# Five weight halves whose low part is a sum made by an accumulating transfer instead of a subtraction on VectorE

## The chip, the core and the metric

The kernel runs on one core of a Trainium2 chip. The metric is the device time of one execution in microseconds. The core has TensorE (matrix products; PE in the profile), VectorE (DVE), ScalarE (ACT), GpSimd (POOL), and SyncE (SP), whose queue issues nearly all transfers. Engines run their own lists of instructions in order and wait for one another only at semaphores.

## The reference

One block of a hybrid encoder: 512 tokens of width 1024, all in float32. A normalised input goes through one wide projection; three branches work on its columns (A, a matrix memory with four heads; B, sparse attention with eight heads; M, attention into 256 memory tokens), and their outputs are merged:

```python
merged = (g[:, :, 0] * (y_a @ w_branch[l, 0])
          + g[:, :, 1] * (y_b @ w_branch[l, 1])
          + g[:, :, 2] * (y_m @ w_branch[l, 2]))
x = x + merged @ w_out[l]
```

The change lies in the products `y_m @ w_branch[2]` and `y_b @ w_branch[1]`.

## The kernel before, in words

**Products in two parts.** TensorE takes operands of a shorter format (fp32r). To keep the precision, each operand is split: the high part is the operand rounded to that format, the low part is what is left. Each product of float32 matrices is then three products: high by high, high by low, low by high. For weights, `w_raw` receives the columns from memory, ScalarE copies them into `w_hi` (`split_hi`, L1472 to L1480), and VectorE subtracts, `w_lo = w_raw - w_hi` (`split_lo`, L2230 to L2234).

**Panels and halves.** A panel is 1024 rows by 512 columns of weights, in two halves `kh` of 512 rows (128 partitions by 2048 elements, 1 MB). `w_raw`, `w_hi` and `w_lo` have one slot for each `kh`. TensorE takes a half in four blocks of 12 products each (`panel`, L830 to L849) and waits ahead of it for the semaphore `w_lo_done`, which counts the low parts in the order of all halves. A slot of `w_hi` and `w_lo` comes free when TensorE has finished the same `kh` of the panel before (`w_used` for kh 0, `proj_done` for kh 1); so while TensorE works on one half, the other is prepared.

**The stage of the change.** After the pairs of B heads come four branch panels, `GB[0]` to `GB[0] + 3`: two for M, two for B. They are called panels 0 to 3 here, and their halves (0,0), (0,1), (1,0) and so on to (3,1). Ahead of panel 0 and in panels 0 to 2, TensorE also does pieces of the last two B heads. Behind each panel VectorE multiplies the four results by gates and adds them up (`branch_merge`, L2737 to L2747). SP loads the next panels (`load`), each half once the low part that was made from the same slot is done, and behind panel 3 it waits for all eight low parts (L757) before it loads the first weights of branch A.

**GpSimd in the stage.** Its last work for B is a power at about 505 us. Then it waits for `ys_lo` to reach `2 * KT`, that is for the low parts of all of B's outputs, and makes four sums of token blocks, `s_full` (L3224 to L3231); the last of eight instructions raises `s_made`. Behind them stand the sums of weights for branch A (`weight_sums`).

**Branch A's first head.** TensorE begins with four operands for queries and keys (`queries_keys`), numbered 0 to 3 here, and goes on with the unit products, operands 4 to 10. Each operand is split as above, by `operand_high` on ScalarE and `operand_low` on VectorE. ScalarE's order in the first head (`a_body`, L2036 on) is: operand 1, a wait for `s_made`, the high part of one sum (`sums_high`, L2033), operand 2, another sum, operand 3, two more sums, then the evacuation `first_tap(0)` (L2000), operand 4 and so on. VectorE's order is: operands 0 to 3 with the merge of panel 3 behind operand 0, the convolution of what `first_tap` left (L2813), operand 4, low parts of the sums (L2874), operands 5 and 6, more convolutions, a sum, operand 7 (L2801).

Of the kernel before, what the change touches and what calls it, by code (L numbers as in the profile page):

```python
# [10 lines left out]
ALU = mybir.AluOpType  # L11
ACT = mybir.ActivationFunctionType
# [9 lines left out]
MT = MEM // P  # L22
# [93 lines left out]
GB = _plan.take(4, 4, (4,) * 4)  # L116
# [40 lines left out]
def hybrid_block(nc, x, mem, positions, norm_g, mem_norm_g, w_in, conv_w, conv_b, mlstm_gate_b,  # L157
# [3 lines left out]
    with ctx:  # L161
        def sb(name, shape, dt=F32):
            return ctx.enter_context(nc.sbuf_tensor(name, shape, dt))

        def sem(name):
            return ctx.enter_context(nc.semaphore(name))
# [4 lines left out]
        w_raw = sb("w_raw", [P, 2, KH, S])  # L171
        w_hi = sb("w_hi", [P, 2, KH, S], F32R)
        w_hi_at = nc.sbuf_base - 4 * 2 * KH * S
        w_lo = sb("w_lo", [P, 2, KH, S], F32R)
# [173 lines left out]
        small2 = sb("small2", [P, 52])  # L348
# [14 lines left out]
        half_turned, half_hi, half_lo = sem("half_turned"), sem("half_hi"), sem("half_lo")  # L363
# [2 lines left out]
        small_landed, vec_landed, ang_landed = sem("small_landed"), sem("vec_landed"), sem("ang_landed")  # L366
        w_landed, idx2_landed = [sem("w_landed0"), sem("w_landed1")], sem("idx2_landed")
        w_hi_done, w_lo_done, w_used = sem("w_hi_done"), sem("w_lo_done"), sem("w_used")
        w_first_cast, w_first_hi, w_first_lo = sem("w_first_cast"), sem("w_first_hi"), sem("w_first_lo")
        idx2_hi_done, idx2_lo_done = sem("idx2_hi_done"), sem("idx2_lo_done")  # L370
        proj_done = [sem(f"proj_done{b}") for b in range(4)]
        bank_empty = [sem(f"bank_empty{b}") for b in range(4)]
# [43 lines left out]
        vec_cols = sem("vec_cols")  # L416
# [395 lines left out]
        def _(pe):  # L812
# [99 lines left out]
            def k_transposes():  # L912
                pe.wait_ge(k_parts, 2)
                pe.wait_ge(gate_steps, 3)
                pe.wait_ge(vec_cols, 2)
                for c in range(2):
                    for t in range(TT):
                        ins = turn(att[1 + c][:, t * P:(t + 1) * P],
                                   k_pair[:, t, c].rearrange("p d n -> p (d n)"), ident[:, :])
                    ins.then_inc(idx_turned, 1)  # L920
# [65 lines left out]
            def first_products(c, m, k0, k1, high=(), low=(), mem_low=(), weights_last=True):  # L986

                orders = (((0, 0), high), ((1, 0), mem_low), ((0, 1), low))
                if not weights_last:
                    orders = (orders[0], orders[2], orders[1])  # L990
                for j, ((a, b), wait) in enumerate(orders):
                    if wait:
                        pe.wait_ge(*wait)
                    for k in range(k0, k1):
                        ins = mm(banks[2 * c + m][:, :], memT[a][:, k, m * P:(m + 1) * P], (w_hi, w_lo)[b][:, c, k % KH, :],
                                 start=(k == 0 and j == 0), stop=(k == KT - 1 and j == 2))
                return ins

            pe.wait_ge(w_first_cast, 1)
            first_products(0, 0, 0, 1, (half_hi, 1), (w_first_lo, 1), (half_lo, 1), weights_last=False)  # L1000
            turn_tile(1)
            first_products(0, 0, 1, 2, (w_first_hi, 1), (w_first_lo, 2))
# [466 lines left out]
        def _(act):  # L1469
            A_ = nc.scalar.activation  # L1470
            steps = Steps(act, act_step)

            def split_hi(p, kh, loads, n, before=None):

                act.wait_ge(w_landed[kh], loads * 16)
                if kh == 1 and before is not None:
                    act.wait_ge(proj_done[before[0]], before[1])
                elif kh == 0 and not (isinstance(p, int) and p == 0):
                    act.wait_ge(w_used, p)
                A_(w_hi[:, kh, :, 0:n], w_raw[:, kh, :, 0:n], ACT.Copy).then_inc(w_hi_done, 1)  # L1480

            def split_y(src, tiles=range(KT)):
                for k in tiles:
                    A_(y_hi[:, k, :], src[:, k * S:(k + 1) * S], ACT.Copy).then_inc(ys_hi, 1)
# [211 lines left out]
            def m_evac(h, first):  # L1696
                for e in range(2):
                    act.wait_ge(proj_done[e], h + (MS[2][e] + 1))
                    if first and e == 0:
                        act.wait_ge(vec_cols, 3)  # L1700
                        act.wait_ge(km_norm_steps, 9)
                    A_(m_qh[:, e, :], banks[e][:, :], ACT.Copy, scale=gqk[:, e:e + 1])
                    A_(m_qfull[:, e, :], banks[e][:, :], ACT.Copy, scale=gqk[:, e:e + 1])
                    ins = A_(m_sq[:, e, :], banks[e][:, :], ACT.Square)
                    ins.then_inc(bank_empty[e], 1)
                for e in range(2):
                    b = 2 + e
                    act.wait_ge(proj_done[b], h + (MS[2][b] + 1))
                    if not first and e == 0:
                        act.wait_ge(m_y, h * 2)  # L1710
                    A_(m_zs[:, e, :], banks[b][:, :], ACT.Silu).then_inc(bank_empty[b], 1)
# [70 lines left out]
            def b_values_high(a):  # L1782

                act.wait_ge(u_added, 6 * (a // 2) + (2 if a % 2 else 6))
                if a:
                    act.wait_ge(b_out, a)
                for half in range(2):
                    ins = A_(b_vh[:, 2 * half:2 * half + 2], b_rawT[a % 2][half][:, :, 2 * P:3 * P], ACT.Copy)
                ins.then_inc(b_vhigh, 1)

            def b_probs_high(a):
                ph = b_pT[0][:, :].rearrange("p (b n) -> p b n", n=P)
                if a % 2 == 0:
                    act.wait_ge(b_rotated, a + 2)
                for t in range(TT):
                    act.wait_ge(b_pturned, a * 4 + (t + 1))
                    if t == 0 and a:
                        act.wait_ge(b_out, a)
                    A_(ph[:, t:4 * t + 1:3, :],
                       att[(t + 2) % 4][:, 0:(t + 1) * P].rearrange("p (s n) -> p s n", n=P), ACT.Copy)\  # L1800
                        .then_inc(b_phigh, 1)

            def b_qk_high(a):
                if a:
                    act.wait_ge(b_scores, 4 * a)
                act.wait_ge(b_turned, a * 2 + 1)
                A_(b_qT[0][:, :], att[0][:, :], ACT.Copy).then_inc(b_qhigh, 1)
                act.wait_ge(b_turned, a * 2 + 2)
                A_(b_kT[0][:, :], att[1][:, :], ACT.Copy).then_inc(b_khigh, 1)
# [110 lines left out]
            split_hi(GB[0] + 1, 0, GB[1] + 2, 512)  # L1920
            b_probs_high(r)
            split_hi(GB[0] + 1, 1, GB[1] + 2, 512, (3, GB[2][3] + 1))
            b_values_high(l)
            b_qk_high(l)
            b_exps(l)
            split_hi(GB[0] + 2, 0, GB[1] + 3, 512)
            b_probs_high(l)
            for k in range(KH):
                yb_high(k)
            split_hi(GB[0] + 2, 1, GB[1] + 3, 512, (3, GB[2][3] + 2))  # L1930
            for k in range(KH, KT):
                yb_high(k)
            split_hi(GB[0] + 3, 0, GB[1] + 4, 512)
            split_hi(GB[0] + 3, 1, GB[1] + 4, 512, (3, GB[2][3] + 3))

            def raw_of(n, first):
                if n == 1 and first:
# [287 lines left out]
        def _(dve):  # L2225
            V = nc.vector
# [3 lines left out]
            def split_lo(p, kh, n):  # L2230

                dve.wait_ge(w_hi_done, p * 2 + (kh + 1))
                V.tensor_tensor(w_lo[:, kh, :, 0:n], w_raw[:, kh, :, 0:n], w_hi[:, kh, :, 0:n].bitcast(F32),  # L2233
                                ALU.subtract).then_inc(w_lo_done, 1)  # L2234
# [73 lines left out]
            V.tensor_copy(memg_col, att[2][:, 0:KT]).then_inc(memg_cols, 1)  # L2308
            dve.wait_ge(memg_cols, 2)
            dve.wait_ge(piece_landed[0], 16)  # L2310
            V.tensor_copy(w_hi[:, 0, 0:1, :], w_raw[:, 0, 0:1, :]).then_inc(w_first_cast, 1)
            dve.wait_ge(w_first_cast, 1)
            piece_low(0)
            mem_low(0)
            piece_low(1)
# [44 lines left out]
            low(10)  # L2360
            low(11)
            split_lo(IDX_PANEL, 0, 512)
            dve.wait_ge(vec_cols, 1)
            V.tensor_copy(cols[:, :], att[2][:, 0:92]).then_inc(vec_cols, 1)
            dve.wait_ge(vec_cols, 2)
            V.tensor_tensor(gqk[:, :], cols[:, 88:90], cols[:, 90:92], ALU.mult).then_inc(vec_cols, 1)

            split_lo(IDX_PANEL, 1, 512)
# [393 lines left out]
            b_probs(r)  # L2762
            for b in (2, 0, 1, 3):
                branch_merge(0, b)
            split_lo(GB[0] + 1, 1, 512)
            b_finish(r)
            b_values_low(l)
            b_qk_low(l)
            b_maxes(l)
            b_scale_p(l)  # L2770
            split_lo(GB[0] + 2, 0, 512)
            b_probs(l)
            for b in range(2):
                branch_merge(1, b)
# [1 line left out]
                yb_low(k)  # L2776
            for b in range(2, 4):
                branch_merge(1, b)
            split_lo(GB[0] + 2, 1, 512)
            b_finish(l)  # L2780
            for k in range(KH, KT):
                yb_low(k)
            split_lo(GB[0] + 3, 0, 512)
            for b in range(4):
                branch_merge(2, b)
            split_lo(GB[0] + 3, 1, 512)


            def raw_of(n, first):
# [314 lines left out]
        def _(pool):  # L3104
            G = nc.gpsimd
# [112 lines left out]
            def a_powers(h):  # L3218
                pool.wait_ge(a_norm_steps, h * 5 + 3)
                G.tensor_tensor(a_den, a_ss, minus_half[:, 0:TT], ALU.pow).then_inc(a_norm_steps, 1)  # L3220

            pool.wait_ge(ys_lo, 2 * KT)

            for f, (k0, t0) in enumerate(((0, HALF_T), (KH, HALF_T), (0, 0), (KH, 0))):  # L3224
# [94 lines left out]
```

## Time and profile before

| what | value |
|---|---|
| median of 3 runs | 958.27 us (957.98 to 958.4) |
| the profiled execution, its time | 957.99 us |
| the profiled execution, its span | 956.2 us |
| TensorE busy | 950.4 us, 99% |
| VectorE busy | 733.0 us, 77% |
| ScalarE busy | 544.8 us, 57% |
| GpSimd busy | 349.0 us, 37% |

The span is the stretch from the first to the last instruction of the profiled execution; 1.8 us of its time lie around it. In the timelines a row is one instruction, or several alike, with its start in microseconds from the start of the span and its duration; in square brackets stands how long the engine was idle before it and what ended the wait. TensorE's rows overlap, since products are pipelined: a row of 0.39 us starts about 0.23 us after the one before.

### The profile page before, as it was taken

To read this page: it belongs to the slowest core of one execution; us is meant where nothing else is said; L and a number is where in the kernel's file an instruction comes from. 1 tells how busy PE (TensorE), PEld (TensorE's weight loads), DVE (VectorE), ACT (ScalarE), POOL (GpSimd) and SP (SyncE) were. 2 spreads that over 40 slices of the span, in tenths; PEclk is the share of its full clock that TensorE was granted. 3 is DMA by queue.
4 is the path that set the end of the run, shared out by engine and by line. 5 is a ranking of instruction groups with operands and counts; after the bars stand their busy time and mean duration, and the time that the engine had idled before them with its cause. 6 is when DMAs were issued, how large, how long until landed. Compare 5 with 4: busy or idle time off the path is not lost. (4 is left out here: it accounts for less than half of the span.)

```text
span 956.2 us, 13763 instructions
## 1 busy us (share of the span) xinstructions
PE 950.4 (99%) x5041; PEld 843.6 (88%) x5041; DVE 733.0 (77%) x1110; ACT 544.8 (57%) x834; POOL 349.0 (37%) x246
## 2 busy tenths in 40 slices
PE   9999999999999999999999999999999999999998
PEld 7888888888989988988988888898998989998877
DVE  6879987688996686685688566896776957984896
ACT  6877644465456546546563422595765857874341
POOL 0200834456327137146120071362613527102910
PEclk9999999999999999999999999999999999999999
DMA  8624222144531631532354335716043150538412
GB/s 293 236 88 132 87 91 71 61 133 133 165 94 61 173 106 53 150 110 72 113 194 172 126 108 157 231 32 200 1 123 109 33 154 1 177 129 306 182 45 88
DMA packets 105158, 119.31 MB, mean 125 GB/s; under 512 B 4772, under 2 KB 80136, under 8 KB 104332
## 3 DMA queue, kind: packets, MB, share of 16 engines
q1 hardware_dynamic: 105084, 118.53, 38.4%
q8 instruction: 36, 0.59, 0.3%
q14 instruction: 22, 0.18, 0.1%
q10 hardware_dynamic: 16, 0.00, 0.0%
HBM read 106.45 MB, written 12.07 MB: 124 GB/s over the span
## 5 line engine op out<-in xcount | busy, mean ns | idle before, releaser
L825 PE MATMUL proj<-hT_hi,w_hi 128*128 128x512 f32 x264 | 104.0, 394 | 0.0
L825 PE MATMUL proj<-hT_hi,w_lo 128*128 128x512 f32 x264 | 103.1, 390 | 0.0
L825 PE MATMUL proj<-hT_lo,w_hi 128*128 128x512 f32 x264 | 102.9, 390 | 0.0
L2233 DVE TENSOR_TENSOR w_lo<-w_raw,w_hi 128x2048 fp32r<-128x2048 f32 x25 | 61.6, 2465 | 44.2 <-ACT w_hi L1480 41.3
L1480 ACT ACTIVATE w_hi<-w_raw 128x2048 fp32r<-128x2048 f32 x24 | 45.9, 1914 | 57.4 <-PE proj L825 55.8
L825 PE MATMUL proj<-y_hi,w_hi 128*128 128x512 f32 x192 | 75.2, 391 | 0.0
L825 PE MATMUL proj<-y_hi,w_lo 128*128 128x512 f32 x192 | 74.8, 390 | 0.0
L825 PE MATMUL proj<-y_lo,w_hi 128*128 128x512 f32 x192 | 74.7, 389 | 0.0
L825 PEld LDWEIGHTS proj<-hT_hi,w_lo 128*128 128x128 f32 x264 | 49.6, 188 | 10.5
L825 PEld LDWEIGHTS proj<-hT_lo,w_hi 128*128 128x128 f32 x264 | 49.6, 188 | 9.9
L825 PEld LDWEIGHTS proj<-hT_hi,w_hi 128*128 128x128 f32 x264 | 49.6, 188 | 9.8
L3170 POOL TENSOR_TENSOR w_raw<-merged,w_raw 128x384 f32<-128x384 f32 x32 | 35.2, 1129 | 55.4 <-DVE w_lo L2584 30.8
L2801 DVE TENSOR_TENSOR w_lo<-w_raw,w_hi 128x1536 fp32r<-128x1536 f32 (+1 forms) x21 | 35.9, 1708 | 22.3 <-ACT w_hi L1967 22.1
L1967 ACT ACTIVATE w_hi<-w_raw 128x1536 fp32r<-128x1536 f32 (+1 forms) x21 | 29.1, 1386 | 40.6 <-DMA w_raw<-w_in_in 13.1
L3242 POOL TENSOR_TENSOR w_raw<-merged,w_raw 128x384 f32<-128x384 f32 x32 | 40.3, 1302 | 29.6 <-DVE w_lo L2801 29.6
L825 PEld LDWEIGHTS proj<-y_hi,w_lo 128*128 128x128 f32 x192 | 36.0, 188 | 7.6
L825 PEld LDWEIGHTS proj<-y_hi,w_hi 128*128 128x128 f32 x192 | 36.1, 188 | 7.4
L825 PEld LDWEIGHTS proj<-y_lo,w_hi 128*128 128x128 f32 x192 | 36.1, 188 | 7.2
L2813 DVE SCALAR_TENSOR_TENSOR negmask<-proj,small,negmask 128x511 f32<-128x511 f32 (+2 forms) x48 | 35.5, 747 | 4.0 <-ACT negmask L2000 2.9
L1319 PE MATMUL proj<-hT_hi,w_hi 128*128 128x512 f32 x96 | 37.6, 392 | 0.0
L1319 PE MATMUL proj<-hT_hi,w_lo 128*128 128x512 f32 x96 | 37.4, 390 | 0.0
L1319 PE MATMUL proj<-hT_lo,w_hi 128*128 128x512 f32 x96 | 37.4, 390 | 0.0
(591 smaller groups left out, 3141.2 us busy)
## 6 DMA issues: line engine op xcount, KB each, us to landing
w_raw<-w_in_in SPq DMA_DIRECT2D x36, 512.0 KB, 4.6
w_raw<-w_in_in SPq DMA_DIRECT2D x56, 256.0 KB, 3.6
w_raw<-w_branch_in SPq DMA_DIRECT2D x12, 1024.0 KB, 5.5
merged<-w_in_in SPq DMA_DIRECT2D x38, 256.0 KB, 3.7
merged<-w_in_in SPq DMA_DIRECT2D x18, 512.0 KB, 5.8
w_raw<-w_mem_kv_in SPq DMA_DIRECT2D x10, 512.0 KB, 6.1
yF<-x_in SPq DMA_DIRECT2D x8, 512.0 KB, 9.9
w_raw<-w_in_in SPq DMA_DIRECT2D x4, 1024.0 KB, 5.3
```

What stands on the lines that cost most here:

```text
L825: ins = mm(ps, lhs[a](k, k0), rhs[b](k, k0), start=(first and k == 0 and j == 0), stop=(last and k == KH - 1 and j == 2))
L1319: ins = mm(banks[b][:, :], w[a][:, k, e * P:(e + 1) * P], hT[b_][:, kh * KH + k, :], start=(kh == 0 and k == 0 and j == 0), stop=(kh == 1 ...
L1480: A_(w_hi[:, kh, :, 0:n], w_raw[:, kh, :, 0:n], ACT.Copy).then_inc(w_hi_done, 1)
L1967: A_(operand(op_hi, n), raw_of(n, first), ACT.Copy).then_inc(op_high, 1)
L2233: V.tensor_tensor(w_lo[:, kh, :, 0:n], w_raw[:, kh, :, 0:n], w_hi[:, kh, :, 0:n].bitcast(F32), ALU.subtract).then_inc(w_lo_done, 1)
L2801: V.tensor_tensor(operand(op_lo, n), raw_of(n, first), operand(op_hi, n).bitcast(F32), ALU.subtract)\
L2813: ins = V.scalar_tensor_tensor(acc[:, lag:], u[:, 0:S - lag], hcw[:, CONV - 1 - lag, b:b + 1], acc[:, lag:], ALU.mult, ALU.add)
L3170: ins = G.tensor_tensor(b_w[out][:, at], b_w[left][:, at], b_w[right][:, at], op)
L3242: ins = G.tensor_tensor(dst[:, at], left[:, at], right[:, at], ALU.subtract)
```

## The change

The low parts of the halves (1,1), (2,0), (2,1), (3,0) and (3,1) are no longer made by VectorE. For each of them:

- ScalarE, right behind the high part, writes the negated high part into the slot of `w_lo` (`split_neg`).
- GpSimd waits for that, and issues a transfer within the on-chip memory that adds `w_raw` to `w_lo`. It then waits until the transfer has landed, and a memset of one element raises `w_lo_done`.
- The five calls of `split_lo` are gone from VectorE's list.

The loop over the five halves stands in GpSimd's list ahead of the wait for `ys_lo` and of `s_full`. The counts of `vec_cols` shift by one because it takes over the part of a semaphore that was dropped.

```diff
+            def split_neg(kh):
+
+                A_(w_lo[:, kh], w_raw[:, kh], ACT.Copy, scale=-1.0).then_inc(half_hi, 1)
...
             split_hi(GB[0] + 1, 1, GB[1] + 2, 512, (3, GB[2][3] + 1))
+            split_neg(1)
             b_values_high(l)
...
             split_hi(GB[0] + 2, 0, GB[1] + 3, 512)
+            split_neg(0)
             b_probs_high(l)
             for k in range(KH):
                 yb_high(k)
             split_hi(GB[0] + 2, 1, GB[1] + 3, 512, (3, GB[2][3] + 2))
+            split_neg(1)
             for k in range(KH, KT):
                 yb_high(k)
             split_hi(GB[0] + 3, 0, GB[1] + 4, 512)
+            split_neg(0)
             split_hi(GB[0] + 3, 1, GB[1] + 4, 512, (3, GB[2][3] + 3))
+            split_neg(1)
...
-            split_lo(GB[0] + 1, 1, 512)
...
-            split_lo(GB[0] + 2, 0, 512)
...
-            split_lo(GB[0] + 2, 1, 512)
...
-            split_lo(GB[0] + 3, 0, 512)
...
-            split_lo(GB[0] + 3, 1, 512)
...
+            for n in range(5):
+                kh = 1 - n % 2
+                pool.wait_ge(half_hi, MT + n + 1)
+                pool.wait_ge(w_lo_done, 2 * GB[0] + 3 + n)
+                G.dma_start(w_lo[:, kh], w_raw[:, kh], accum_op=ALU.add).then_inc(sums_landed, 16)
+                pool.wait_ge(sums_landed, 16 * (n + 1))
+                G.memset(small2[0:1, 51:52], 0.0).then_inc(w_lo_done, 1)
+
             pool.wait_ge(ys_lo, 2 * KT)
```

GpSimd's list before, from the last power of branch B (L3206) to the first sums of weights of branch A (L3242):

```order
80 L3206 TENSOR_TENSOR small<-small,minus_half 128x8
81 L3226 TENSOR_TENSOR arena<-hT_hi,hT_lo 128x1024 x4
82 L3228 TENSOR_TENSOR arena<-arena 128x1024
83 L3229 TENSOR_TENSOR arena<-arena 128x1024
84 L3230 TENSOR_TENSOR arena<-arena 128x1024
85 L3231 TENSOR_TENSOR arena<-arena 128x1024
86 L3242 TENSOR_TENSOR w_raw<-w_raw 128x384 x4
```

The same place now (line numbers are 5 to 13 higher in the changed kernel):

```order
80 L3211 TENSOR_TENSOR small<-small,minus_half 128x8
81 L3231 DMA w_lo<-w_raw 128x2048
82 L3233 MEMSET small 1x1
...
89 L3231 DMA w_lo<-w_raw 128x2048
90 L3233 MEMSET small 1x1
91 L3239 TENSOR_TENSOR arena<-hT_hi,hT_lo 128x1024 x4
92 L3241 TENSOR_TENSOR arena<-arena 128x1024
93 L3242 TENSOR_TENSOR arena<-arena 128x1024
94 L3243 TENSOR_TENSOR arena<-arena 128x1024
95 L3244 TENSOR_TENSOR arena<-arena 128x1024
```

The eight instructions of `s_full` moved behind five transfers and five memsets, the last of which belongs to half (3,1).

ScalarE's list before, from the high part of half (2,1) to the first operand of branch A (L1967) and the first sum (L2033):

```order
320 L1480 ACTIVATE w_hi<-w_raw 128x2048
321 L1905 ACTIVATE y_hi<-yF 128x512 x2
322 L1905 ACTIVATE y_hi<-arena 128x512
323 L1905 ACTIVATE y_hi<-sig 128x512
324 L1480 ACTIVATE w_hi<-w_raw 128x2048 x2
325 L1967 ACTIVATE w_hi<-w_raw 128x1024 x2
326 L2033 ACTIVATE y_hi<-arena 128x1024
```

The same place now:

```order
322 L1481 ACTIVATE w_hi<-w_raw 128x2048
323 L1485 ACTIVATE w_lo<-w_raw 128x2048
324 L1910 ACTIVATE y_hi<-yF 128x512 x2
325 L1910 ACTIVATE y_hi<-arena 128x512
326 L1910 ACTIVATE y_hi<-sig 128x512
327 L1481 ACTIVATE w_hi<-w_raw 128x2048
328 L1485 ACTIVATE w_lo<-w_raw 128x2048
329 L1481 ACTIVATE w_hi<-w_raw 128x2048
330 L1485 ACTIVATE w_lo<-w_raw 128x2048
331 L1977 ACTIVATE w_hi<-w_raw 128x1024 x2
332 L2043 ACTIVATE y_hi<-arena 128x1024
```

Behind each high part stands one more pass over the half, into `w_lo`; the rest keeps its place.

## Rows read from the trace of the kernel before

**Rows 1.** The page's span line and busy time of each engine, whole run.

```profile
span 956.2 us, 13763 instructions
PE 950.4 (99%) x5041; PEld 843.6 (88%) x5041; DVE 733.0 (77%) x1110; ACT 544.8 (57%) x834; POOL 349.0 (37%) x246
```

**Rows 2.** The windows view of three stretches: busy us (instructions) of each engine.

```profile
core 0: us, PE busy (x) PEld busy (x) DVE busy (x) ACT busy (x) POOL busy (x), PEclk, DMA share, GB/s
560.00:570.00 10.00, 10.00 (x46) 8.29 (x45) 8.01 (x5) 1.89 (x1) 9.84 (x4) 1.00 0.01 2
610.00:620.00 10.00, 10.00 (x53) 9.26 (x52) 9.92 (x11) 5.29 (x6) 4.04 (x4) 1.00 0.49 161
620.00:630.00 10.00, 10.00 (x60) 10.00 (x59) 9.90 (x8) 7.45 (x11) 10.00 (x7) 1.00 0.00 0
```

**Rows 3.** The timeline of TensorE, first products of each step: start us, us, what.

```profile
534.88 0.39 PE L825 MATMUL proj<-y_hi,w_hi 128*128 128x512 f32 x1
546.92 0.39 PE L1167 MATMUL att<-b_ph,b_vh 128*128 128x512 f32 x1
559.72 0.39 PE L825 MATMUL proj<-y_hi,w_hi 128*128 128x512 f32 x1
570.60 0.39 PE L825 MATMUL proj<-y_hi,w_hi 128*128 128x512 f32 x1
581.48 0.39 PE L825 MATMUL proj<-y_hi,w_hi 128*128 128x512 f32 x1
603.24 0.39 PE L1319 MATMUL proj<-hT_hi,op_hi 128*128 128x512 f32 x1
626.63 0.34 PE L1340 MATMUL att<-w_hi,y_hi 128*128 128x384 f32 x1
```

**Rows 4.** The timeline of ScalarE, high parts of the five halves.

```profile
519.48 1.92 ACT L1480 ACTIVATE w_hi<-w_raw 128x2048 fp32r<-128x2048 f32 x1 [4.96 <-PE proj L825]
535.84 1.91 ACT L1480 ACTIVATE w_hi<-w_raw 128x2048 fp32r<-128x2048 f32 x1
547.17 1.92 ACT L1480 ACTIVATE w_hi<-w_raw 128x2048 fp32r<-128x2048 f32 x1 [2.88 <-PE proj L825]
559.98 1.92 ACT L1480 ACTIVATE w_hi<-w_raw 128x2048 fp32r<-128x2048 f32 x1 [6.76 <-PE proj L825]
570.86 1.92 ACT L1480 ACTIVATE w_hi<-w_raw 128x2048 fp32r<-128x2048 f32 x1 [8.96 <-PE proj L825]
```

**Rows 5.** The timeline of VectorE, subtractions of the last two halves.

```profile
561.93 4.20 DVE L2233 TENSOR_TENSOR w_lo<-w_raw,w_hi 128x2048 fp32r<-128x2048 f32 x1 [7.50 <-ACT w_hi L1480]
577.29 2.28 DVE L2233 TENSOR_TENSOR w_lo<-w_raw,w_hi 128x2048 fp32r<-128x2048 f32 x1
```

**Rows 6.** The DMA view's issues: tiles, queue, count, KB each, us to landing.

```profile
w_raw<-w_branch_in SPq DMA_DIRECT2D x12, 1024.0 KB, 5.5
out_b<-w_out_in SPq DMA_DIRECT2D x4, 1024.0 KB, 12.2
```

**Rows 7.** The timeline of GpSimd, sums of token blocks, the first five and the last.

```profile
554.50 9.47 POOL L3226 TENSOR_TENSOR arena<-hT_hi,hT_lo 128x1024 f32<-128x1024 f32 x4 [47.53 <-DVE y_lo L2736]
564.05 4.32 POOL L3228 TENSOR_TENSOR arena<-arena 128x1024 f32<-128x1024 f32 x1
574.08 2.74 POOL L3231 TENSOR_TENSOR arena<-arena 128x1024 f32<-128x1024 f32 x1
```

**Rows 8.** The timeline of ScalarE after the last half.

```profile
593.58 1.05 ACT L2033 ACTIVATE y_hi<-arena 128x1024 fp32r<-128x1024 f32 x1
601.78 0.76 ACT L2000 ACTIVATE negmask<-proj,small 128x512 f32<-128x512 f32 x1
```

**Rows 9.** The timeline of VectorE, two steps of branch A's first head.

```profile
602.58 2.31 DVE L2813 SCALAR_TENSOR_TENSOR negmask<-proj,small,negmask 128x511 f32<-128x511 f32 x3 [1.34 <-ACT negmask L2000]
624.63 1.75 DVE L2801 TENSOR_TENSOR w_lo<-w_raw,w_hi 128x1536 fp32r<-128x1536 f32 x1
```

**Rows 10.** The source view of L2874, low parts of the four sums.

```profile
L2874 DVE TENSOR_TENSOR y_lo<-arena,y_hi x4: 1212/1908/2054, 608.9 to 622.0; 128x1024 fp32r<-128x1024 f32 x4
```

More of the change, by code:

```diff
@@ L368, in hybrid_block @@
         w_hi_done, w_lo_done, w_used = sem("w_hi_done"), sem("w_lo_done"), sem("w_used")
-        w_first_cast, w_first_hi, w_first_lo = sem("w_first_cast"), sem("w_first_hi"), sem("w_first_lo")
+        w_first_hi, w_first_lo = sem("w_first_hi"), sem("w_first_lo")
+        sums_landed = sem("sums_landed")
         idx2_hi_done, idx2_lo_done = sem("idx2_hi_done"), sem("idx2_lo_done")
@@ L914, in k_transposes @@
                 pe.wait_ge(gate_steps, 3)
-                pe.wait_ge(vec_cols, 2)
+                pe.wait_ge(vec_cols, 3)
                 for c in range(2):
@@ L997, in first_products @@
                 return ins
-            pe.wait_ge(w_first_cast, 1)
+            pe.wait_ge(vec_cols, 1)
             first_products(0, 0, 0, 1, (half_hi, 1), (w_first_lo, 1), (half_lo, 1), weights_last=False)
@@ L1699, in m_evac @@
                     if first and e == 0:
-                        act.wait_ge(vec_cols, 3)
+                        act.wait_ge(vec_cols, 4)
                         act.wait_ge(km_norm_steps, 9)
@@ L2310, in _ @@
             dve.wait_ge(piece_landed[0], 16)
-            V.tensor_copy(w_hi[:, 0, 0:1, :], w_raw[:, 0, 0:1, :]).then_inc(w_first_cast, 1)
-            dve.wait_ge(w_first_cast, 1)
+            V.tensor_copy(w_hi[:, 0, 0:1, :], w_raw[:, 0, 0:1, :]).then_inc(vec_cols, 1)
+            dve.wait_ge(vec_cols, 1)
             piece_low(0)
@@ L2362, in _ @@
             split_lo(IDX_PANEL, 0, 512)
-            dve.wait_ge(vec_cols, 1)
+            dve.wait_ge(vec_cols, 2)
             V.tensor_copy(cols[:, :], att[2][:, 0:92]).then_inc(vec_cols, 1)
-            dve.wait_ge(vec_cols, 2)
+            dve.wait_ge(vec_cols, 3)
             V.tensor_tensor(gqk[:, :], cols[:, 88:90], cols[:, 90:92], ALU.mult).then_inc(vec_cols, 1)
```

## The prediction, made before the changed kernel was run

> **What bounds the kernel now.** I read first the busy times of the page: TensorE is busy for 950.4 of 956.2 us, 99% [rows 1]. So no change beside TensorE can win more than the 5.8 us in which it is not busy, and what has to be asked of this change is whether TensorE will have to wait where it doesn't now. Second, the windows view: in the stretch of the branch panels TensorE is busy for 10.00 of 10 us at a granted clock of 1.00 (the higher level, 2.4 GHz), VectorE for 8.01, ScalarE for 1.89; and in branch A's first head VectorE is busy for 9.92 and 9.90 of 10 us [rows 2]. That second stretch matters below: VectorE has no room there. Third, the timelines, for the time between the moment at which an operand can be begun and the moment at which TensorE takes it.
>
> The slack of each of the five halves is the start of its high part on ScalarE [rows 4] against TensorE's start on it [rows 3]. (1,1): 519.48 to 534.88, 15.4 us. (2,0): 535.84 to 546.92 (TensorE waits for the low part ahead of the B head's products that stand there), 11.1 us. (2,1): 547.17 to 559.72, 12.6 us. (3,0): 559.98 to 570.60, 10.6 us. (3,1): 570.86 to 581.48, 10.6 us. Today the chain in it is 1.92 us for the high part and 2.28 for the subtraction, which for (3,0) took 4.20 us since GpSimd worked beside it [rows 5].
>
> **The change, step by step.** It takes five subtractions from VectorE, four of some 2.3 us and one of 4.20. None of them is waited for by TensorE, so this gives nothing by itself.
>
> *ScalarE* gets five passes over the same 128 by 2048 elements, 1.92 us each as the pass in front of each; both are finished about 3.8 us after the high part begins. What is queued behind (copies for the last B head, high parts of B's outputs) is moved by 1.9 us in a stretch in which ScalarE was busy for 1.89 of 10 us, so I put it at nothing. If that cover is gone, it costs up to 1.9 us once.
>
> *The transfer.* The trace has no transfer issued by GpSimd and none that accumulates, so its time D, from GpSimd's wait to the landing, must be bounded. Below: a plain transfer of the same 1024 KB lands after 5.5 us [rows 6], and the new one moves as much and must read its destination too. Above: the slowest rows of that size took 12.2 us [rows 6]; three passes over the bytes (two reads, a write) at the plain price would be 16.5 us. I take 8.5, the plain 5.5 and about half of it again for the second read and GpSimd's own issue: it is nearer to the row of the same size than to the queue of four big loads. With 0.3 us for the semaphores and the memset, a half is ready F = 3.8 + 8.5 + 0.3 = 12.6 us after its high part begins (9.6 at the lower bound, 16.3 and 20.6 at the upper two). *A page on it:* the Trainium skill's "Collectives: The Full Stack", section "The bandwidth ceiling: the fold count and why AG ≠ RS ≠ AR", says that a reduction in the transfer engines reads two sources over the same ring and so gets half the rate of a copy; no run before this one shows it. By the fixed 2.0 us and the rate that the Trainium skill's "DMA: Bandwidth & Descriptors" gives in "Anatomy of one DMA — SWDGE (gpsimd) path", with twice the bytes read, an estimate is 2.0 + 2 x 2.4 = 6.8 us, which would make D 1.7 us smaller and the forecast 3.4 us lower.
>
> *TensorE in the stage.* (1,1) holds (12.6 under 15.4). (2,0) misses its slack by 12.6 - 11.1 = 1.5 us. (2,1) holds. (3,0) misses by 12.6 - 10.6 = 2.0 us. (3,1) has 10.6 and those 2.0 us, 12.6, and just holds. So TensorE has lost 3.5 us at (3,1), and the last low part is done at 570.86 + 1.5 + 12.6 = 585.0 us, where it was 577.29 + 2.28 = 579.6.
>
> *What stands behind the transfers on GpSimd.* This is the larger term. The eight sums of token blocks began at 554.50, when B's outputs were ready, and ended at 574.08 + 2.74 = 576.8 [rows 7]: 22.3 us, with 16.8 us to spare until ScalarE used them at 593.58 [rows 8]. Now they stand behind all five transfers, whose last ends at 585.0. Their length: L3226 took 9.47 / 4 = 2.4 us each; eight such are 19.0, the lower bound; the stretch seen with VectorE in between is 22.3, the upper. I take 21. `s_made` then comes at 606.0, and ScalarE, whose list is in order, stands before it from operand 1 on. Behind the wait come a sum, operand 2, a sum, operand 3, two sums: six passes. In steps of the starts (593.58 to 594.53 is 0.95 us) [rows 8] they take 6 x 0.95, about 5.8 us with the hand-over, the operands having been loaded meanwhile, so `first_tap(0)`, at 601.78 in the trace, starts at 611.8, 10.0 us later. VectorE's convolution follows it (602.58 before) [rows 9], and from there to operand 7, whose low part starts at 624.63 and is done at 626.38 [rows 9], VectorE is busy nearly without a gap [rows 2], so it cannot catch up. TensorE takes operand 7 at 626.63 [rows 3], 0.25 us after it is done. So TensorE, which by then has 3.5 us of delay from the stage and may lose some more at operand 2 (603.24 [rows 3]), is brought to a delay of 10.0 - 0.25 = 9.8 us in all. The earlier stalls are contained in this, not added to it. In short: the delay is 2F + 559.8 (the last low part) + 21 + 5.8 - 601.78 - 0.25, or 2F - 15.4; it moves by 2 us for each 1 us of D.
>
> *The sum.* Profiled execution: span 956.2 + 9.8 = 966.0, and 1.8 us around it (957.99 less 956.2) make 967.8. The median of the runs stands 0.3 us above that execution, so 968.1 us, 1.0% slower. A measurement of this kernel tells about 0.2%, 1.9 us, from no change.
>
> **Rivals.** *Only the transfers count* (VectorE makes good the late sums). Speaks for it: some of VectorE's time in the first head is waiting for GpSimd, a low part of a sum takes from 1.21 to 2.05 us for the same shape [rows 10]; against it: 9.9 of 10 us busy. Then the cost is the stalls in the stage, 3.5 us, and operand 2: `s_made` 606.0, a sum and the high part 2.0, the low part 1.2, is 609.2, against 603.24 + 3.5 = 606.7, 2.5 us more. 6.0 us, 964.3.
>
> *The transfer is much slower* (D of 12.2 to 16.5). For it: nothing here shows how fast the adding runs. With F = 16.3 (1,1) misses by 0.9, the delay is about 2 x 16.3 - 15.4 + 0.9 = 18 us, 976; with F = 20.6 nearly every half waits for the one before it and it is some 28 us, 986. Loads of the next halves and gates run beside the transfers and could push D this way.
>
> *Not slower.* One mechanism: the transfer lands like a plain one, D = 5.5, F = 9.6, so no half is late, and the stretch of the sums is free of VectorE's subtractions. `s_made` is then at 570.86 + 9.6 + 19.0 = 599.5, `first_tap(0)` at 605.3, 3.5 us late; if VectorE gets back the conflicts with GpSimd in 608 to 624, as these rows' spread allows (two low parts at up to 0.8 us each [rows 10], the rest in others), about 2.2 us, and the 0.25, TensorE waits 1.1 us: 959.4. It decides from D under about 6 us; a win beyond that is excluded, since TensorE has no idle time in the stage to give back. *Beside it,* the Trainium skill's "SBUF — State Buffer", section "SBUF: two separate sides", says that VectorE and GpSimd lock a shared port pair against each other; the 4.20 us of (3,0) against 2.28 [rows 5] agree, and it is what this rival would live on.
>
> **How the numbers follow.** Forecast (both terms, D from 7 to 11): 0.60. Only the transfers: 0.12. Much slower transfer: 0.21. Not slower: 0.07, of which 0.05 within 0.2% and 0.02 faster by noise in the placement of loads. The forecast's own range is D from 7 (965) to 11 (973) with the sums 2 us to either side: 963 to 975. To hold 8 in 10, I reach down to 961, between the not slower case and the transfers alone, and up to 982, into the much slower one. Faster by over 0.2%: 0.02; within: 0.05; slower: 0.93.
>
> **What the changed profile would show.** Idle time of TensorE ahead of L825 in the stage, released by GpSimd's memset: about 1.5 us at half (2,0) and 2 us at (3,0), none at (1,1) and (2,1). `w_hi` and `w_lo` passes of 1.92 us back to back on ScalarE. GpSimd's sums starting near 585 and not 554.5. ScalarE idle some 10 us ahead of L2043, released by GpSimd, and TensorE idle at operands 1 or 2 and again at operand 7 behind VectorE. I am wrong if D is under 6 us, if the sums don't hold up ScalarE, or if TensorE waits somewhere else, for instance for gates that SP loads later because its list waits for a low part.

## The result: 10.4 us slower, and the profile after

| | median us | range, runs | span of the profiled execution |
|---|---|---|---|
| before, on the same chip | 958.12 | 957.98 to 958.4, 4 | 956.2 |
| changed | 968.55 | 967.85 to 969.61, 4 | 966.2 |

The ratio of the changed kernel's time to that before is 1.0108, with a 95% interval of 1.0096 to 1.0121. The forecast was 968.1 us. The page of the changed kernel, its span line, busy times and the issue of the new transfers (KB each, median us from issue to landing), against [rows 1] and [rows 6]:

```profile
span 966.2 us, 13778 instructions
PE 953.3 (99%) x5041; PEld 844.8 (87%) x5041; DVE 724.6 (75%) x1105; ACT 554.0 (57%) x839; POOL 350.3 (36%) x256
w_lo<-w_raw POOLq DMA_DIRECT2D x5, 1024.0 KB, 7.8
```

VectorE has 8.4 us less work, and the span is 10.0 us longer. TensorE has the same 5041 products, so what has to be found is where it stopped. The waits view of TensorE names it (us in total, times, longest):

```profile
PE proj L1320 <- DVE w_lo L2806: 5.9, 1, 5.9
...
PE proj L826 <- POOL small L3233: 1.5, 1, 1.5
```

Both are new; the waits left out stand before the change too. The timeline of TensorE, first products of steps as in [rows 3], and two more of operand 1:

```profile
546.87 0.50 PE L1168 MATMUL att<-b_ph,b_vh 128*128 128x512 f32 x1
...
572.35 0.50 PE L826 MATMUL proj<-y_hi,w_hi 128*128 128x512 f32 x1 [1.53 <-POOL small L3233]
...
605.79 0.79 PE L1320 MATMUL proj<-hT_hi,w_hi 128*128 128x512 f32 x1 [5.95 <-DVE w_lo L2806]
...
606.81 0.63 PE L1320 MATMUL proj<-hT_hi,w_lo 128*128 128x512 f32 x1
607.24 0.63 PE L1320 MATMUL proj<-hT_hi,w_hi 128*128 128x512 f32 x1
...
613.04 0.39 PE L1320 MATMUL proj<-hT_hi,op_hi 128*128 128x512 f32 x1
...
636.64 0.41 PE L1341 MATMUL att<-w_hi,y_hi 128*128 128x384 f32 x1
```

Each row less its partner of before is TensorE's shift: 0 at (2,0), 1.75 at (3,0) (572.35 against 570.60), 9.80 at operand 2 (613.04 against 603.24), 10.01 at operand 7 (636.64 against 626.63), and nothing is added after that. Between operand 1 and operand 2 lies a second loss: the products start 0.43 us apart (606.81 to 607.24), not 0.23. The windows view, columns as in [rows 2]:

```profile
560.00:570.00 10.00, 10.00 (x46) 8.28 (x45) 4.06 (x6) 3.72 (x2) 0.86 (x1) 1.00 1.01 301
...
600.00:606.00 6.00, 0.21 (x1) 0.21 (x2) 5.70 (x4) 1.39 (x2) 4.50 (x2) 0.72 0.00 0
606.00:608.00 2.00, 2.00 (x5) 1.61 (x6) 1.23 (x1) 1.57 (x2) 0.00 (x0) 0.50 0.54 145
608.00:610.00 2.00, 2.00 (x7) 1.52 (x6) 0.00 (x0) 0.57 (x1) 0.00 (x0) 0.64 0.93 272
...
620.00:630.00 10.00, 10.00 (x54) 9.30 (x53) 9.93 (x11) 5.18 (x6) 4.16 (x5) 1.00 0.50 166
```

Behind the 5.95 us of idleness the granted clock is at 0.50, the lower level of 1.2 GHz, until about 609.4: products start 0.43 us apart there, and the shift grows by 1.8 us, from 7.99 behind the wait (605.79 against 597.80) to 9.80. VectorE is still full in the first head (9.93 of 10 us). In 560 to 570 it has the half of its work (4.06 us), and the transfer engines, idle before, are full (1.01). Not all of that is the new transfer: SP's list has the load of a half, which waits for a low part, in front of the loads of the gates, so these start at 559.51 us and not at 551.87. VectorE waits for them (first row of its timeline below), TensorE doesn't.

The timeline of GpSimd, against [rows 7]: two of the five transfers with the memset behind each, the last memset, and the sums.

```profile
539.74 0.87 POOL L3231 DMA_DIRECT2D w_lo<-w_raw  x1 [8.40 <-ACT w_lo L1485]
546.73 0.09 POOL L3233 MEMSET small<- 1x1 f32 x1 [6.12 <-DMA w_lo<-w_raw]
...
564.05 0.86 POOL L3231 DMA_DIRECT2D w_lo<-w_raw  x1 [5.00 <-ACT w_lo L1485]
572.21 0.09 POOL L3233 MEMSET small<- 1x1 f32 x1 [7.30 <-DMA w_lo<-w_raw]
...
582.97 0.09 POOL L3233 MEMSET small<- 1x1 f32 x1 [7.18 <-DMA w_lo<-w_raw]
583.03 10.43 POOL L3239 TENSOR_TENSOR arena<-hT_hi,hT_lo 128x1024 f32<-128x1024 f32 x4
593.54 2.73 POOL L3241 TENSOR_TENSOR arena<-arena 128x1024 f32<-128x1024 f32 x1
...
601.91 2.67 POOL L3244 TENSOR_TENSOR arena<-arena 128x1024 f32<-128x1024 f32 x1
```

From the start of a transfer's row to its memset 7.0 to 8.2 us pass. The sums start 28.5 us later than before (583.03 against 554.50) and end at 604.58. The timeline of ScalarE, a pair of passes of the stage and the way to `first_tap(0)` (now L2010), against [rows 4] and [rows 8]:

```profile
560.04 1.92 ACT L1481 ACTIVATE w_hi<-w_raw 128x2048 fp32r<-128x2048 f32 x1 [7.18 <-PE proj L826]
561.86 1.90 ACT L1485 ACTIVATE w_lo<-w_raw 128x2048 fp32r<-128x2048 f32 x1
...
604.61 1.06 ACT L2043 ACTIVATE y_hi<-arena 128x1024 fp32r<-128x1024 f32 x1 [9.05 <-POOL arena L3244]
...
609.43 1.06 ACT L1977 ACTIVATE w_hi<-w_hi_f 128x1024 fp32r<-128x1024 f32 x1 [1.86 <-DMA w_hi_f<-w_in_in]
...
612.30 0.76 ACT L2010 ACTIVATE negmask<-proj,small 128x512 f32<-128x512 f32 x1
```

And VectorE, where the wait at operand 1 comes from; the last two rows answer to [rows 9]:

```profile
564.92 0.69 DVE L2755 TENSOR_TENSOR tabs<-proj,tabs 128x512 f32<-128x512 f32 x1 [11.10 <-DMA tabs<-sig_kept]
...
594.65 2.17 DVE L2757 TENSOR_TENSOR merged<-merged,tabs 128x512 f32<-128x512 f32 x1
...
600.26 2.12 DVE L2757 TENSOR_TENSOR merged<-merged,tabs 128x512 f32<-128x512 f32 x1
602.31 2.31 DVE L2827 COPY small<-cols 128x20 f32<-128x20 f32 x1
604.53 1.21 DVE L2806 TENSOR_TENSOR w_lo<-w_raw,w_hi 128x1024 fp32r<-128x1024 f32 x1
...
613.09 2.32 DVE L2818 SCALAR_TENSOR_TENSOR negmask<-proj,small,negmask 128x511 f32<-128x511 f32 x3 [1.34 <-ACT negmask L2010]
...
634.80 1.75 DVE L2806 TENSOR_TENSOR w_lo<-w_raw,w_hi 128x1536 fp32r<-128x1536 f32 x1
```

Before the change, in the timeline of VectorE, a merge of panel 2, which ran beside GpSimd's sums, and the last rows of panel 3, for which GpSimd had finished them:

```profile
566.76 2.17 DVE L2747 TENSOR_TENSOR merged<-merged,tabs 128x512 f32<-128x512 f32 x1
...
593.35 0.69 DVE L2747 TENSOR_TENSOR merged<-merged,tabs 128x512 f32<-128x512 f32 x1
593.96 0.17 DVE L2822 COPY small<-cols 128x20 f32<-128x20 f32 x1
594.04 1.22 DVE L2801 TENSOR_TENSOR w_lo<-w_raw,w_hi 128x1024 fp32r<-128x1024 f32 x1
```

The additions of the merge of panel 3 take 2.17 us beside GpSimd's sums and took 0.69; a copy of 20 columns takes 2.31 and took 0.17. The merge that starts at 594.65 ends at 596.82, 0.55 us after the sum beside it (593.54 + 2.73 = 596.27); the merge at 600.26 ends at 602.38, 0.55 us after the sum in front of the row at 601.91, which ended at 601.83 (599.16 + 2.67). So each waits until GpSimd's instruction is over. The longer additions are not new in themselves: before the change the merge of panel 2 paid for them (2.17 us at 566.76), where no product waited for VectorE; now it is panel 3's, and the low part of operand 1 stands behind it. It comes at 604.53, against 594.04; 1.8 us of that are there before the merge, since operand 0's low part starts at 588.78 and not at 587.01.

So the first reading is this: the sums behind the transfers delay TensorE twice, by VectorE at operand 1 (5.95 us and the lower clock, which brings the shift to 9.80) and by ScalarE and VectorE at operand 7 (10.01), and the stage's own 1.75 us is contained in both. The experiments have to show that the order on GpSimd is the cause, that there are two bounds of nearly one height, and what the adding costs.

### The profile page after: what moved, and what is told of

The parts are those of the page before. It is cut to its first block and busy times, and to the rows that moved or that the text cites. A ratio compares the mean times of both kernels' runs of the same rounds, so it can differ in the third digit from the quotient of the medians.

```text
span 966.2 us, 13778 instructions
## 1 busy us (share of the span) xinstructions
PE 953.3 (99%) x5041; PEld 844.8 (87%) x5041; DVE 724.6 (75%) x1105; ACT 554.0 (57%) x839; POOL 350.3 (36%) x256
## 5 line engine op out<-in xcount | busy, mean ns | idle before, releaser
L2243 DVE TENSOR_TENSOR w_lo<-w_raw,w_hi 128x2048 fp32r<-128x2048 f32 x20 | 48.3, 2417 | 33.5 <-ACT w_hi L1481 30.7
L826 PEld LDWEIGHTS proj<-hT_hi,w_lo 128*128 128x128 f32 x264 | 49.5, 188 | 10.5
```

Of the source, the lines that this page charges most:

```text
L826: ins = mm(ps, lhs[a](k, k0), rhs[b](k, k0), start=(first and k == 0 and j == 0), stop=(last and k == KH - 1 and j == 2))
```

## The experiments

Ratios are against the kernel before, run on the same chip. "Shift" is TensorE's start on a product less the start before the change.

### order_only: the order without the transfers

The kernel before, with GpSimd held back ahead of its sums until half (3,1) is ready:

```diff
+            pool.wait_ge(w_lo_done, 2 * (GB[0] + 4))
             pool.wait_ge(ys_lo, 2 * KT)
```

> The kernel before, with all low parts still subtracted on VectorE and no transfer by GpSimd; only GpSimd's sums of token blocks wait until the last of the eight low parts is done, so they start near 579.6 us and not at 554.5. Theory (the position of the sums in GpSimd's list is the main term): the sums end near 601, first_tap(0) starts some 7 us late, TensorE waits at operand 1, and the time is 963 to 966 us (5 to 8 us over the kernel before). Rival (the transfers are the cost, late sums are absorbed): within 1 us of the kernel before.

Measured: 962.14 us (961.08 to 963.09), before 958.23, ratio 1.0039 (1.0025 to 1.0052): 3.9 us, below the 963 to 966 that I expected. The timelines of GpSimd (last sum), ScalarE (`first_tap(0)`) and TensorE (operand 7):

```profile
593.64 2.73 POOL L3232 TENSOR_TENSOR arena<-arena 128x1024 f32<-128x1024 f32 x1
604.66 0.76 ACT L2000 ACTIVATE negmask<-proj,small 128x512 f32<-128x512 f32 x1
629.32 0.45 PE L1340 MATMUL att<-w_hi,y_hi 128*128 128x384 f32 x1 [2.01 <-issue]
```

Without GpSimd's sums beside it the subtraction for (3,0) was quick, so the last low part was there at 575.1 and not at 579.6 as I had assumed. `first_tap(0)` is 2.9 us late and TensorE 2.69 at operand 7; behind its wait of 2.0 us the clock falls again and the shift grows to 4.34. The wait at operand 1 that I had expected did not come (0.3 us there): the merges took 2.17 us beside the sums here too, but VectorE began operand 0's low part at 582.78, 6.0 us ahead of the changed kernel. So the late sums alone, with no transfer in the kernel, hold up TensorE at operand 7, as the prediction had it, and not at operand 1. With sums that begin 7.9 us later still it would be more; the next run shows it from the other side.

### between: all five transfers, the sums not behind them

The changed kernel, with the first four instructions of the sums put around the issue of the fourth transfer, two behind them ahead of the fifth, and the last two beside it:

```diff
+            for n in range(3):
+                sum_start(n)
+                sum_end(n)
             pool.wait_ge(ys_lo, 2 * KT)
+            block_sum(0)
+            block_sum(1)
+            sum_start(3)
...
+            sum_end(3)
...
+            sum_start(4)
...
+            sum_end(4)
```

> All five transfers as in the changed kernel, but the eight instructions of the sums of token blocks are issued between the issue and the landing of the fourth and fifth transfer and in the gaps around them, so that the last sum is done near 581 to 583 us. Theory: only the transfer's own term is left, the wait of 1.5 us (1.75 us of delay) at half (3,0), perhaps 1 us more from conflicts on GpSimd: 959.5 to 961.5 us. Rival (transfers and contention are the cost): 966 to 969 us as the changed kernel.

Measured: 961.5 us (961.18 to 962.25), ratio 1.0036 (1.0022 to 1.005). Against the changed kernel's 968.55 this is 7.0 of the 10.4 us, and only the order on GpSimd differs. The sums end at 582.0, and TensorE's waits are those of the stage, 1.9 us at (3,0), and 0.3 at operand 7:

```profile
PE proj L826 <- POOL small L3235: 1.9, 1, 1.9
...
PE att L1341 <- issue: 0.3, 1, 0.3
```

The time is at the upper edge of the 959.5 to 961.5 that I expected. The shift is 2.8 us behind the stage and 3.3 from operand 7 on. The 0.5 us that operand 7 adds come from half (3,1), ready at 584.0: SP loads the first weights of branch A only behind it, and ScalarE waits 3.4 us for those of operand 3 (2.4 before), so `first_tap(0)` is 3.8 us late.

### operand1_early: the wait at operand 1 taken away

The changed kernel, with VectorE's low part of operand 1 put ahead of the last two merges of panel 3:

```diff
             operand_low(0, 0, True)
-            for b in range(4):
+            for b in range(2):
+                branch_merge(3, b)
+            operand_low(1, 0, True)
+            for b in range(2, 4):
                 branch_merge(3, b)
...
```

> The changed kernel, but VectorE makes the low part of operand 1 behind two of the four merges of panel 3 instead of behind all four, so TensorE's wait of 5.95 us at operand 1, and the half clock behind it, should go or shrink to a wait of 2 to 3 us at operand 2. Theory (ScalarE's and VectorE's chain from the late sums to operand 7 decides, the earlier waits are contained in it): the same as the changed kernel within 1 us, 967.5 to 969.5. Rival (the ladder of waits adds up: 5.95 us at operand 1 and 1.8 us of low clock are costs of their own): 961 to 965 us.

Measured: 967.16 us (967.05 to 967.63), ratio 1.0095 (1.0079 to 1.011), which overlaps that of the changed kernel; the span is 1.0 us shorter (965.2). That is the "same" that I expected or 1 us less, and nowhere near the rival. TensorE's waits:

```profile
PE proj L1320 <- DVE op_lo L2806: 2.6, 1, 2.6
PE att L1341 <- issue: 1.7, 1, 1.7
PE proj L826 <- POOL small L3237: 1.6, 1, 1.6
...
PE proj L1320 <- DVE w_lo L2806: 0.3, 1, 0.3
```

The largest wait of the changed kernel went from 5.95 to 0.3 us, and what was given back is taken at operand 2 (2.6 us, and the lower clock behind it again) and at operand 7 (1.7). The shift at operand 7 is 9.04: the second bound is there without the first. ScalarE's six passes, which now had no load to wait for, took 605.61 to 611.32, 5.7 us. That is where the 1.0 us comes from, although the sums ended 1.0 us later than in the changed kernel (605.58).

### scalar_free: ScalarE's wait for the sums taken away too

operand1_early, and ScalarE's wait for the sums moved behind `first_tap(1)`:

```diff
                 first_tap(1, h)
+                if first:
+                    act.wait_ge(s_made, A_SMADE + 1)
+                    act.wait_ge(proj_done[3], GB[2][3] + 4)
+                    for f in (1, 2, 3, 0):
+                        sums_high(f)
...
```

> The changed kernel with its late sums, but nobody stands behind them: ScalarE takes the high parts of the four sums behind first_tap(1) and not between the operands, and VectorE makes operand 1 behind two merges. Theory (the route is ScalarE's list from the wait for the sums to first_tap(0)): the operands come in time, what is left is VectorE held up by GpSimd in 585 to 604 us and the 1.75 us of half (3,0), first_tap(0) and its convolution some 2 to 5 us late: 961 to 964 us. Rival (VectorE's and GpSimd's conflict, not the wait in ScalarE's list, makes the delay): 966 us or more.

Measured: 963.4 us (963.21 to 964.07), ratio 1.0055 (1.0041 to 1.0068), as expected, and 3.8 us under operand1_early, from which it differs only in the place of ScalarE's wait. `first_tap(0)` starts at 605.91, and the shift is 1.76 at (3,0), 3.76 at operand 2, 4.92 at operand 7. GpSimd's sums lie as late as in the changed kernel, so their lateness is paid for where ScalarE's list stands before them; what stays beside the stage's 1.76 us is VectorE, whose merges still take 2.17 us each beside them (`first_tap(0)` itself waited 1.09 us for it; timeline of VectorE):

```profile
596.70 3.41 DVE L2802 TENSOR_TENSOR w_lo<-w_raw,w_hi 128x1024 fp32r<-128x1024 f32 x1
...
600.74 2.17 DVE L2753 TENSOR_TENSOR merged<-merged,tabs 128x512 f32<-128x512 f32 x1
```

### plain_copy: the price of adding

The changed kernel, with the transfer copying and not adding (the low parts are then the whole weights; the sum is left out). One execution.

```diff
-                G.dma_start(w_lo[:, kh], w_raw[:, kh], accum_op=ALU.add).then_inc(sums_landed, 16)
+                G.dma_start(w_lo[:, kh], w_raw[:, kh]).then_inc(sums_landed, 16)
```

> The changed kernel with plain copies of w_raw over the negated high part in place of the five adding transfers, so the low parts are replaced by the whole weights and the sum is left out of the computation. Theory (the second read makes an adding transfer slower): the landing is 2 us or more sooner than the 7.0 to 8.2 us of the adding ones, at 5 to 6 us. Rival (issue and completion make up the difference to the 5.5 us of plain loads): 7 us or more, as the adding ones.

The DMA view's row, and the source view's times to landing with the row of the issuing instruction:

```profile
w_lo<-w_raw POOLq DMA_DIRECT2D x5, 1024.0 KB, 5.1
L3231 POOL DMA_DIRECT2D w_lo<-w_raw x5: 537/538/768, 523.7 to 575.1; - x5
DMA to landing us min/median/max: 4.2/5.1/5.6
```

The same view of the changed kernel:

```profile
L3231 POOL DMA_DIRECT2D w_lo<-w_raw x5: 862/862/1070, 523.4 to 574.9; - x5
DMA to landing us min/median/max: 6.9/7.8/8.1
```

Adding costs 2.7 us of 7.8, and 0.32 us more at the issue. The plain copy holds every half in time (no wait in the stage), and its time is still 966.81, span 965.0: the sums begin at 580.83, TensorE waits 5.4 us at operand 1, and then has the lower clock for 6.2 us, which takes the shift from 5.82 to 8.79 (windows view):

```profile
603.60:609.80 6.20, 6.18 (x15) 4.84 (x16) 2.45 (x2) 4.47 (x5) 0.00 (x0) 0.50 0.80 231
```

At operand 7 it doesn't wait. So with each transfer 2.7 us quicker only 1.2 us of the span come back.

### neg_first: the transfer started earlier

The changed kernel, with ScalarE's negated pass ahead of the high part, so that the transfer runs beside the high part's pass; GpSimd also waits for the high part ahead of its memset.

```diff
-            split_hi(GB[0] + 3, 1, GB[1] + 4, 512, (3, GB[2][3] + 3))
-            split_neg(1)
+            split_both(GB[0] + 3, 1, GB[1] + 4, (3, GB[2][3] + 3))
...
+                pool.wait_ge(w_hi_done, 2 * GB[0] + 4 + n)
```

> The changed kernel, but ScalarE writes the negated high part before it writes the high part, so each transfer is issued 1.8 us sooner and the high part is made beside it. Everything else, GpSimd's order too, as in the changed kernel. Theory: half (3,0) is ready some 10.3 us after ScalarE starts on it, inside its slack of 10.6, so the wait there (1.53 us in the changed kernel) goes, and the last low part, the sums behind it and the delay at operand 7 come some 1.8 us sooner: 966 to 967.5 us, the waits at operand 1 and the low clock behind it stay. Rival (the waits for the transfers are the main cost): 961 to 963 us.

Measured: 968.27 us (967.55 to 968.71), ratio 1.0105 (1.009 to 1.0121): not told apart from the changed kernel, and the expectation was missed. The last transfer starts 1.96 us earlier and lands 0.5 us earlier (timeline of GpSimd):

```profile
572.97 0.86 POOL L3232 DMA_DIRECT2D w_lo<-w_raw  x1 [1.96 <-ACT w_lo L1490]
582.47 0.09 POOL L3235 MEMSET small<- 1x1 f32 x1 [8.64 <-DMA w_lo<-w_raw]
```

In both kernels SP issues a store of 1 MB (`merged_kept`) at 572.6 to 572.7, and the transfer engines are full until 581; in this one their share is 1.11, 1.06 and 0.98 in the three windows of 2 us from 575, in the changed kernel 1.00, 1.14 and 0.98. That the landing is set by this sharing and not by the start fits both, but it is not shown: no run took the store away. In neg_first_between, below, the store is issued 4.3 us after the transfer starts, and the transfer's memset comes 8.28 us after that start; here the store is issued 0.4 us ahead of it, and the memset comes after 9.50 us. What the earlier start did give is in the stage: TensorE waits 0.4 us twice (0.8 in all) and not 1.5. Behind it the shift at operand 7 is 9.50 for 10.01, the 0.5 us of the landing, so it is the landing that I had wrong here and not the route from it.

### neg_first_between and three_halves: the versions that cost least

Two kernels: all five transfers, with the orders of neg_first and between together; and the changed kernel with transfers for (1,1), (2,0) and (2,1) alone, VectorE subtracting for (3,0) and (3,1):

```diff
+            dve.wait_ge(w_lo_done, 2 * GB[0] + 6)
+            split_lo(GB[0] + 3, 0, 512)
             for b in range(4):
                 branch_merge(2, b)
+            split_lo(GB[0] + 3, 1, 512)
...
-            for n in range(5):
+            for n in range(3):
```

> All five transfers, with the negated high part written first and the sums of token blocks issued between and beside the fourth and fifth transfer. Theory: no half is late and the sums are done near 580 us, so what is left is a later landing of branch A's first weights (last low part near 581 us, against 579.6): 958.2 to 960 us. Rival (the transfers cost by contention, whatever their order): 961 us or more.

> Transfers for the halves (1,1), (2,0) and (2,1) alone; the low parts of (3,0) and (3,1) are subtracted on VectorE, which first waits until (2,1) is done. GpSimd's sums start near 559 us, end near 581, and are used at 593.6. Theory: both terms are gone, 957.8 to 959 us, the same as the kernel before. Rival (any transfer in the stage costs by contention with loads): 1 us or more over the kernel before.

Measured: 959.97 us (958.59 to 960.94), ratio 1.0018 (1.0009 to 1.0027), and 958.63 us (957.67 to 959.75), ratio 1.0005 (0.9996 to 1.0014); both as expected. In the first, all five low parts still come by transfer and 8.6 of the 10.4 us are gone; 0.6 us of waiting in the stage is left, and a shift of 1.19. In the second GpSimd's sums run from 558.3 to 583.1, 6.3 us later than before and still ahead of ScalarE's use at 593.66, and no shift is over 0.1 us. Three subtractions fewer on VectorE gain nothing. TensorE doesn't wait in this stage before the change, so no order of these transfers can beat that kernel, and none did.

## Why the prediction was right, step by step

- **The transfer, D.** Taken 8.5 us, measured 7.0 to 8.2. Its bounds came from plain transfers that SP issued [rows 6]; the plain one from GpSimd took 5.1, and adding 2.7 more, close to the "about half again". F, from the high part's start to the memset, was 11.1 to 12.3 us and not 12.6.
- **The stage.** Of the two forecast stalls, (2,0) did not come: its memset stood at 546.73, TensorE at 546.87, a slack of 11.1 used up to 0.1 us. (3,0) cost 1.53 for the forecast 2.0. (1,1), (2,1) and (3,1) held, as said. 3.5 us were forecast and 1.75 lost.
- **The sums.** Length 21 taken, 21.55 measured; begun at 583.0 and not 585.0; `s_made` at 604.6 and not 606.0.
- **Six passes.** 5.8 us forecast, 7.7 measured, since operand 3's weights landed late and ScalarE waited 1.86 us. I had said that they would have been loaded meanwhile. Where that wait is absent (operand1_early) they took 5.7. This error and the one in the transfer have opposite signs, 1.9 against 1.4 us, and `first_tap(0)` came at 612.30 for the forecast 611.8. The total is nearer than its terms are.
- **VectorE saturated up to operand 7.** Right: 10.5 us late at `first_tap(0)`, 10.2 at the low part (634.80 against 624.63), 10.01 at TensorE. The earlier stalls are contained, as said.
- **Not seen in its size.** I named a possible wait at operands 1 or 2, and priced none for the forecast. It is 5.95 us with 1.8 us of lower clock behind it, a shift of 9.80, 0.2 us under the other bound. It was hidden under it by chance, and the second idle time that I had forecast, at operand 7, shrank to that 0.21 us. The step that was missing: GpSimd's sums don't only end later, they now run beside VectorE's merges, which went from 0.69 to 2.17 us. The rows to see it from were there, the 4.20 against 2.28 us in [rows 5]. Those merges alone don't make the wait: in order_only VectorE has the same ones but starts on them earlier, and operand 1 waits 0.3 us.
- **"2 us for each 1 us of D".** Not borne out at the lower end. One of the two stands for half (2,0) being late, and by the prediction's own sum that needs F over 11.1, D over 7.0; its transfer took just 7.0, so it was not late, and 1 us for 1 us is what was left. Nor is it the bound at operand 7 that holds there. With 2.7 us less, plain_copy came out of the wait at operand 1 with a shift of 5.82 for 7.99, and its longer time at the lower clock took back 1.2 of these 2.2 us before operand 2 (3.0 for 1.8). The 1.0 left and the 0.2 us that operand 7 no longer adds are the 1.2 us of the span.
- **The gates.** I had named TensorE waiting for gates loaded late as a sign of being wrong. They were loaded 7.6 us later and VectorE waited 11.1 us for them, but no product did.
- **The rivals.** Only the transfers count: 6.0 us was wrong for the changed kernel, since VectorE did not catch up. The not slower one needed D under 6; plain_copy has D = 5.6 at most and is 8.5 us slower than before, so this rival was wrong in its mechanism too, not only in its D: it had the sums 19.0 us long, and they took 21.6 (580.83 to 602.41), and it had no wait at operand 1. The much slower transfer is out by the landing times.

## What to carry to other kernels

Work moved to an engine that "has time" stands in that engine's list in front of whatever it did there before; ask first who uses what is now behind it, and put the waiting instruction where nothing is queued (order_only: 3.9 us with no other change; between: 7.0 of 10.4 us given back by order alone). If a step is moved in time, look also at what it now runs beside, and price that neighbour again. And when one wait is found in a profile, take it away before calling it the cause: here 5.95 us of it, with the lower clock behind, were worth about 1.

## What the runs showed of the hardware

- An on-chip transfer of 1 MB issued by GpSimd lands after 4.2 to 5.6 us as a copy (plain_copy) and 6.9 to 8.1 as a sum (changed kernel; up to 8.6 in operand1_early and 9.5 in neg_first); GpSimd is held 0.54 and 0.86 us by the issue. *A page on it:* the Trainium skill's "Collectives: The Full Stack", section "The bandwidth ceiling: the fold count and why AG ≠ RS ≠ AR", puts a reduction at half the rate of a copy. The traces show 1.5 times the copy's time, 7.8 against 5.1 us, each counted whole from issue to landing; they don't show the rate apart from what issue and completion take.
- Beside GpSimd's sums, VectorE's additions of two operands from on-chip memory wait for the end of GpSimd's instruction (2.17 for 0.69 us), and so did a copy of 20 columns (2.31 for 0.17), while `tabs<-proj,tabs`, one of whose operands is a product's result, keeps its 0.68. *A page on it:* the Trainium skill's "SBUF — State Buffer", section "SBUF: two separate sides", calls it a lock that is held for the whole instruction; the ends 0.55 us after GpSimd's agree. In the kernel named between one merge took 5.51 us.
- TensorE's granted clock was at the lower level behind waits of 6.1 (neg_first), 5.95, 5.42 (plain_copy), 2.6 (operand1_early) and 2.0 us (order_only), 0.50 to 0.54 in the 3 us behind each, and at 1.00 behind those of 1.5 to 1.9 us. Each time it cost 1.5 to 3.0 us beyond the wait itself (shift before and after the slow products).
